# First block of a two-block model: retention heads and neighbourhood-attention heads in pairs, decay blocks made once, weight rounding in two halves

## The reference, cut to what matters

```
proj = hn @ w_in                      # rq rk rv rg nq nk nv, 512 columns each
rq, rk = rotary(rq), rotary(rk) / 8
y   = retention(rq, rk, rv)           # 8 heads of 64: (q k^T) * gamma^|i-j|, one gamma
                                      # forwards, one backwards, times v
y   = group_norm(y) * g * silu(rg)
na  = neighbourhood_attention(nq, nk, nv, bias)   # 8 heads of 64, softmax over 256 keys
out = concat(y, na) @ w_out
```

## Time and profile before

| | |
|---|---|
| median of 3 runs | 1109.04 us (1108.8 to 1109.66) |
| the profiled execution: time, span | 1107.25 us, 1105.5 us |
| TensorE busy, weight loads | 1022.7 us (93%), 897.2 us |
| VectorE, ScalarE, GpSimd busy | 519.2, 607.8, 688.2 us |
| mean granted TensorE clock | 0.960 of 2.4 GHz |
| DMA | 178.68 MB, 162 GB/s in the mean |

### The profile page before, as it was taken

One profiled execution on the slowest core, in us unless ns is written; L12 is line 12 of the kernel. 1 busy time (PEld: TensorE's weight loads), 2 busy tenths in 40 slices (PEclk: granted clock), 3 DMA queues, 4 the chain that ended last, 5 costly groups with the idle time before them and its releaser, 6 DMA issues. The chain is left out here.

```text
span 1105.5 us, 16084 instructions
## 1 busy us (share of the span) xinstructions
PE 1022.7 (93%) x6261; PEld 897.2 (81%) x6261; DVE 519.2 (47%) x988; ACT 607.8 (55%) x969; POOL 688.2 (62%) x546
## 2 busy tenths in 40 slices
PE   5999797999999899899988689999997999999988
PEld 4897576999999688788867579999996887787877
DVE  3934614545444546386752545545444225114443
ACT  6443535655555566586845455555556467755531
POOL 3976324665757477676746655665675963866464
PEclk9999688999999899899988789999998999999999
DMA  9773212666454465554523345555455654743320
GB/s 320 242 211 131 98 39 86 225 231 230 163 191 150 130 191 158 188 168 155 192 95 118 130 134 191 174 189 200 162 189 160 155 189 150 231 132 135 116 76 38
DMA packets 131945, 178.68 MB, mean 162 GB/s; under 512 B 21457, under 2 KB 94045, under 8 KB 131677
## 3 DMA queue, kind: packets, MB, share of 16 engines
q1 hardware_dynamic: 127693, 169.95, 47.2%
q10 hardware_dynamic: 4176, 7.71, 2.2%
HBM read 176.51 MB, written 5.24 MB: 164 GB/s over the span
## 5 line engine op out<-in xcount | busy, mean ns | idle before, releaser
L496 POOL TENSOR_TENSOR wlo<-raw,whi 128x512 fp32r<-128x512 f32 x510 | 668.5, 1346 | 399.6 <-ACT whi L1123 399.6
L1123 ACT ACTIVATE whi<-raw 128x2048 fp32r<-128x2048 f32 (+1 forms) x150 | 283.5, 1893 | 191.1 <-PE PS L513 134.2
L511 PE MATMUL PS<-Th,whi 128*128 128x256 f32 (+1 forms) x1008 | 289.9, 288 | 2.8 <-POOL wlo L496 1.4
L512 PE MATMUL PS<-Tl,whi 128*128 128x256 f32 (+1 forms) x1008 | 287.3, 285 | 0.0
L513 PE MATMUL PS<-Th,wlo 128*128 128x256 f32 (+1 forms) x1008 | 287.1, 285 | 0.0
L508 PE MATMUL PS<-whi,Th 128*128 128x512 f32 (+1 forms) x512 | 208.7, 408 | 13.1 <-DVE Tl L1615 6.2
L510 PE MATMUL PS<-whi,Tl 128*128 128x512 f32 (+1 forms) x512 | 201.7, 394 | 0.0
L509 PE MATMUL PS<-wlo,Th 128*128 128x512 f32 (+1 forms) x512 | 201.6, 394 | 0.0
L511 PEld LDWEIGHTS PS<-Th,whi 128*128 128x128 f32 (+1 forms) x1008 | 194.1, 193 | 8.8 <-issue 4.1
L1670 DVE SCALAR_TENSOR_TENSOR arena<-PS,cols,arena 128x255 f32<-128x255 f32 (+1 forms) x272 | 118.6, 478 | 168.0 <-ACT arena L1222 155.2
L512 PEld LDWEIGHTS PS<-Tl,whi 128*128 128x128 f32 (+1 forms) x1008 | 194.3, 193 | 1.3 <-issue 0.5
(11 more groups left out here) (216 smaller groups left out, 1117.1 us busy)
## 6 DMA issues: line engine op xcount, KB each, us to landing
raw<-in_ffn_w_up_dram SPq DMA_DIRECT2D x44, 1024.0 KB, 5.1
raw<-in_ffn_w_down_dram SPq DMA_DIRECT2D x22, 1024.0 KB, 4.9
raw<-in_w_in_dram SPq DMA_DIRECT2D x22, 1024.0 KB, 5.0
raw<-in_c_w_in_dram SPq DMA_DIRECT2D x16, 1024.0 KB, 5.3
raw<-in_ab_w_in_dram SPq DMA_DIRECT2D x14, 1024.0 KB, 7.3
raw<-in_c_w_out_dram SPq DMA_DIRECT2D x8, 1024.0 KB, 4.9
raw<-in_ab_w_out_dram SPq DMA_DIRECT2D x4, 1024.0 KB, 4.9
raw<-in_c_w_in_dram SPq DMA_DIRECT2D x8, 512.0 KB, 5.3
```

What stands on the lines that cost most here:

```text
L496: i = nc.gpsimd.tensor_tensor(wlo[n % NLO][:, c:e], raw[n % NRAW][:, c:e], whi[n % NHI][:, c:e].bitcast(F32), ALU.subtract)
L511: mm(o, wh, ah, start=first, stop=False)
L512: mm(o, wh, al, start=False, stop=False)
L1123: act.activation(whi[n % NHI][:, 0:width], raw[n % NRAW][:, 0:width], ACT.Copy)\
```

## The change

1. Slots: `rg` comes before `nv`; the NA bias loads go ahead of slot `nv 0`, which is one place later in SyncE's queue. `rg` is made in banks 2 and 3, `nv` in 0 and 1.
2. `high(n)` rounds in two instructions of half a slot each; the first signals `w_hi_half`, on which GpSimd starts the first half of its subtractions.
3. Retention in pairs: the scores of two heads are sent alternately, half a `fm` slot follows (`halves`), then both outputs. VectorE multiplies each head in two operations of 256 columns.
4. The decay blocks of all heads are made once: the 128x128 blocks off the diagonal by 16 exponentials on ScalarE with a scale from a column, the diagonal ones by three wide VectorE operations and three exponentials. They lie in free room of the arena, in `sqj` and in `gpost`, so the load of `gpost` moves behind the retention.
5. NA with the function `pairs` of the second block, made general: scores of two heads alternately, then hooks with half or whole slots (`nv`, `mo0`), then transposes and values. The gate of the retention output is worked out before NA as far as it does not need `rg`. The NA output is turned in two parts (`turn_na`), the second inside `out_last`.

```diff
-        tm("nv", win, 3072)
         tm("rg", win, 1536)
+        tm("nv", win, 3072)
...
-                if n == slot_no[("nv", 1)]:
+                if n == slot_no[("nv", 0)]:
...
-                pool.wait_ge(*at("w_hi", n))
+                pool.wait_ge(*at("w_hi_half", n))
...
+                step = min(512, width // 2)
+                for c in range(0, width, step):
+                    e = c + step
+                    if c == width // 2:
+                        pool.wait_ge(*at("w_hi", n))
...
-            for h in range(NH + 1):
-                if h < NH:
-                    ret_scores(h)
-                if h >= 1:
-                    ret_out(h - 1)
-                if h == 1:
-                    slot_fm(("nq", 1), 3)
-                elif h in (2, 3):
-                    slot_fm(("nk", h - 2), h - 2)
-                elif h in (4, 5):
...
+            for p in range(NH // 2):
+                ret_scores(p)
+                if p < 2:
+                    slot_fm(("nq", 1), 3, halves=(p,))
+                else:
+                    if p == 2:
+                        pe.wait_ge(*read(("rv", 1)))
+                    slot_fm(("nk", 0), 0, halves=(p - 2,))
+                ret_out(2 * p)
+                ret_out(2 * p + 1)
+            slot_fm(("nk", 1), 1)
+            pe.wait_ge(*read(("nq", 1)))
+            block_tm("rg", 2)
...
+                for p in range(n + 1):                       # pairs, TensorE
+                    if p < n:
+                        if p:
+                            pe.wait_ge(*at("a_sc", (tag, 2 * p - 1)))
+                        for t in range(NT):
+                            for i in (2 * p, 2 * p + 1):
+                                o = mm(PS[:, 4 + i % 2, ...], q(t), k(nk), start=True, stop=True)
+                        hook(p, "a")
+                        turn(2 * p)
+                    if p:
+                        values(2 * p - 2)
+                        values(2 * p - 1)
+                    if p < n:
+                        hook(p, "m")
+                        turn(2 * p + 1)
+                    hook(p, "b")
...
+                  keyed({(0, "a"): (lambda: na_value(0),), (0, "b"): (lambda: na_value(1), turn_ret), (1, "a"): (mo_first,),
+                         (2, "a"): (lambda: out_slot("mo0", 1, 10, ("y0a", 3), halves=(0,)),),
+                         (3, "a"): (lambda: out_slot("mo0", 1, 10, ("y0a", 3), halves=(1,)),),
+                         (3, "b"): (lambda: turn_na(0),)}))
+            out_last("mo0", 4, (12, 14), [("y0b", 1), ("y0b", 3)], mid=lambda: turn_na(2))
...
-                    act.activation(whi[n % NHI][:, 0:width], raw[n % NRAW][:, 0:width], ACT.Copy)\
-                        .then_inc(*done("w_hi", n))
+                    hf = width // 2
+                    act.activation(whi[n % NHI][:, 0:hf], raw[n % NRAW][:, 0:hf], ACT.Copy).then_inc(*done("w_hi_half", n))
+                    act.activation(whi[n % NHI][:, hf:width], raw[n % NRAW][:, hf:width], ACT.Copy).then_inc(*done("w_hi", n))
...
+            for h, (a, b) in enumerate(dcy_at):              # ScalarE, behind set_up
+                act.activation(dcy3[a][:, b, 0:P], pfb[:, 1, S:S + P], ACT.Exp, scale=lg[:, 8 + h:9 + h])
+                i = act.activation(dcy3[a][:, b, S:S + P], pfb[:, 0, P:S], ACT.Exp, scale=lg[:, h:h + 1])
...
+            for a, h, n in ((0, 0, 5), (1, 5, 1), (2, 6, 2)):
+                act.activation(dcy3[a][:, :, P:S], darg[0][:, h:h + n, :], ACT.Exp).then_inc(*done("r_d", a))
...
+            pairs("na", 4, False, keyed({                    # ScalarE; U(x) rounds up to three slots behind x
+                (0, "m"): (U(("nv", 0)),), (0, "b"): (value_copy, U(("nv", 1)), lambda: T_hi("y0a", 4, 8, 2, lambda k: col("gn", k))),
+                (1, "m"): (U(("mo0", 0)),), (3, "m"): (U(("mo0", 1)),), (3, "b"): (lambda: T_hi("y0b", 2, 12, 4, lambda k: None),)}))
...
-                lk(ts(dcy[h % 2], pfb[:, 1, :], lg[:, 8 + h:9 + h], None, ALU.mult))
-                stt3(out=dcy[h % 2], in0=pfb[:, 0, :], scalar=lg[:, h:h + 1], in1=dcy[h % 2], op0=ALU.mult, op1=ALU.add)\
-                    .then_inc(*done("r_arg", h))
...
+            for k in range(2):
+                i = tt(darg[k], bc(pfb[:, 1 - k, 0:P], 1, NH), bc(lg[:, 8 - 8 * k:16 - 8 * k], 2, P), ALU.mult)
+            lk(i)
+            tt(darg[0], darg[0], darg[1], ALU.add).then_inc(*done("r_arg"))
...
+            ret_var()
+            ret_scale()
+            pairs("na", 4, False, lambda i, t: nabias[:, i, 128 - 128 * t:384 - 128 * t], na_write,
+                  keyed({(0, "a"): (ret_gate,), (1, "x"): (lambda: T_lo("y0a", 4, 8, 2, lambda k: col("gn", k)),),
+                         (3, "b"): (lambda: T_lo("y0b", 2, 12, 4, lambda k: None),)}))
```

More of the change, by code:

```diff
@@ L547, in slot_fm, with slot_dn @@
                                   k == 0, k == KD - 1, False)
-                i.then_inc(*done("w_used", n))
-            def slot_dn(name, ah, al, first, b0=4, mid=None):
+                if 1 in halves:
+                    i.then_inc(*done("w_used", n))
+            def slot_dn(name, ah, al, first, b0=4, mid=None, halves=(0, 1)):
                 n = slot_no[name]
-                pe.wait_ge(*low(n))
+                if 0 in halves:
+                    pe.wait_ge(*low(n))
                 h, l = whi[n % NHI], wlo[n % NLO]
-                order = [(k, t, hf) for k in range(2) for t in range(NT) for hf in range(2)]
+                order = [(k, t, hf) for k in halves for t in range(NT) for hf in range(2)]
                 for j, (k, t, hf) in enumerate(order):
@@ L561, in slot_dn, with last_two @@
                               first and k == 0, False, True)
[L562 to L564 removed]
+                if 1 in halves:
+                    i.then_inc(*done("w_used", n))
+            def last_two(names, acts, ready, b0=4, mid=None):
                 ns = [slot_no[name] for name in names]
@@ L731, in values @@
-                    n.then_inc(*done("a_v", (tag, i)))
-                n = len(heads)
-                for i in range(n + 2):
-                    if i < n:
-                        scores(i)
-                    if 1 <= i <= n:
-                        turn(i - 1)
-                    if i >= 2:
-                        values(i - 2)
-                    after(i)
-            def operands(h, qT, kT, kk, v, causal):
-                b = (h % 2) * DH
-                return (lambda t: qT[b:b + DH, h // 2, t * P:(t + 1) * P], lambda nk: kT[b:b + DH, kk, 0:nk], v, causal)
@@ L747, in _ @@
-            pe.wait_ge(*read(("nv", 1)))
-            pe.wait_ge(*at("gn_c", 1))
-            def also(table):
-                def f(i):
-                    for g in table.get(i, ()):
-                        g()
-                return f
+                        for c in range(t + 1 if causal else NT):
+                            a = (i // 2 % 2) * 256 + t * P + (i % 2) * DH
+                            o = mm(PS[:, 7, a:a + DH], pt[i % 2][:, 2 * t + c, :], heads[i][2](c), start=c == 0, stop=c == (t if causal else NT - 1))
@@ new lines, in keyed, with f, operands, na_value @@
+            def keyed(table):
+                def f(p, place):
+                    for g in table.get((p, place), ()):
+                        g()
+                return f
+            def operands(h, qT, kT, kk, v):
+                b = (h % 2) * DH
+                return (lambda t: qT[b:b + DH, h // 2, t * P:(t + 1) * P], lambda nk: kT[b:b + DH, kk, 0:nk], v)
+            def na_value(hf):
+                if hf == 0:
+                    pe.wait_ge(*read(("nk", 1)))
+                slot_tm(("nv", hf), 0, 4 * hf, hf == 0, hf == 1)
@@ L1327, in also @@
-            def also(table):
-                def f(i):
-                    for g in table.get(i, ()):
-                        g()
-                return f
-            def later(name):
-                return lambda: high(slot_no[name] + 3)
-            high(slot_no[("rg", 1)] + 3)
-            attention("na", NH, False, also({0: (ret_gate,), 3: (lambda: T_hi("y0a", 4, 8, 0, lambda k: col("gn", k)),), 5: (later(("mo0", 0)),),
-                                             8: (later(("mo0", 1)),)}))
@@ L1821, in ret_var, with keyed, f, na_write @@
+            def keyed(table):
+                def f(p, place):
+                    for g in table.get((p, place), ()):
+                        g()
+                return f
+            def na_write(p, rc, o):
+                return tt(hn[:, :, 512 + P * p:512 + P * (p + 1)].rearrange("p t (h d) -> p t h d", h=2), o, bc(rc, 3, DH), ALU.mult)
             def ret_var():
```

444 lines of the change are left out of this document (173 added, 271 removed).

## The result

The changed kernel takes 1083.97 us (median of 4 runs, 1082.29 to 1086.53); beside it the kernel before took 1109.35 us (1108.8 to 1109.76). The ratio is 0.9767, 95% interval 0.9739 to 0.9794: 25.4 us less. I use these two where sizes matter: 25.2 us. By this median the time lies just inside the range, so that the miss of its end is small; the 19.8 us of gain were short by 5.4 all the same.

What follows compares the result with a forecast made beforehand. TensorE was taken to set the time, waiting in the first block's NA. 0.4 + 2.8 + 18.2 - 2.5 + 0.9 = 19.8 us off the median of 1109.04 gave 1089.3 us, range 1084.5 to 1097.0.

Steps and rivals of the forecast that it cites:

- Net elsewhere: gain 0.9: Rounding in halves, beyond the start: 2.4 us less waiting for GpSimd against 1.5 us of later roundings; bounds -2 and +2.4.
- 0.4 us at the start: Rounding in halves: TensorE's 0.48 us wait for GpSimd at 22.58 us goes, minus 0.1 us for VectorE's first slot.
- retention: Retention in pairs: 3.15 us fewer scores and a 0.77 us wait gone, less a 1.1 us stall: gain 2.8 us.
- NA and its clock (18.2 - 2.5): NA in pairs: 11.6 us idle, 4.2 scores and 7.5 low clock removed, 5.1 new idle added; 2.5 lost to the clock.
- the new gap: NA, near 118 us: TensorE stands 3.5 us for ScalarE and VectorE; the clock falls to 1.2 GHz, 2.5 us lost.
- The mask stall: Retention, third pair: VectorE's two masks while GpSimd works make TensorE wait 1.1 us; bounds 0 and 2.2.
- (1): NA: the clock does not fall in the 3.5 us gap, 2.5 us more gain: 1086.8 us, chance 0.15.
- (2): Retention: ScalarE is late, with decay exponentials of 0.5 us and masks under GpSimd's work: 1094.3 us, chance 0.16.
- (3): NA: the clock stays low through the pairs until 140 us, costing 8.5 instead of 2.5 us: 1095.3 us, chance 0.06.
- (4): Retention and NA scores: interleaved pairs don't run side by side, price 7.4 us: 1096.7 us, chance 0.04.
- (5): Slots after the first block: halves make ScalarE the bound, 0.2 us on each, and the kernel slower: 1115.1 us, chance 0.03.
- (6): Slots behind the change: the gain is given back as they wait for rounding or loads: 1109 us, chance 0.02.

Runs made afterwards that it cites:

- whole roundings: The changed kernel with each slot rounded in one ScalarE instruction again, run in two groups: 1087.99 us by median.
- gate ahead: The changed kernel with NA heads singly in the old order, the retention output's gate still worked out before NA: 1096.75 us.
- gate inside: The changed kernel with single NA heads and the retention output's root, tanh copies and gating products put back inside NA: 1104.1 us.
- doubled exponentials: The changed kernel with the sixteen 128x128 exponentials of the decay blocks issued twice, with the same values: 1085.46 us.
- Halves only up to layer 1: The changed kernel with slots rounded in halves only before the first slot of the state-space layer, whole from there on: 1086.94 us.
- high parts first: The changed kernel with ScalarE's four high parts of the retention output moved ahead of the next slot's rounding: 1081.14 us.

## Why the forecast was off, step by step

**What failed: "Net elsewhere: gain 0.9" of the rounding in halves,** and with it the assumption that beyond NA nothing moves but idle time. With the 0.4 us at the start the forecast gave the halves 1.3 us; they are worth 3.3 us on the changed kernel and 3.6 on the one before. I had counted both sides as idle time: waits for GpSimd (up to 2.4) against roundings ahead of a wait (1.5). Both sides were too small. The runs show 5.0 us for the second operation alone and 5.6 to 8.3 us for the earlier start, with TensorE's idle time the same within 1.1 us. What moves beside it is the time at 1.2 GHz. The rest of the change was short as well: the kernel before against whole roundings makes 21.9 us (interval 19.7 to 23.6), and the forecast's terms without the halves 18.5. The bounds -2 and +2.4 stood on idle time as well, so the range was too narrow at this point.

**The ladder.** By medians: before 1109.9; halves 1106.3 (-3.6); retention in pairs, decay blocks once and the order of slots 1104.1 (-2.2); gate ahead of NA 1096.75 (-7.35); NA in pairs 1084.7 (-12.1).

| step | forecast | by medians | by the two timelines |
|---|---|---|---|
| halves (0.4 + 0.9) | 1.3 | 3.6 | 1.2 at the start |
| retention | 2.8 | 2.2 | 4.4 |
| NA and its clock (18.2 - 2.5) | 15.7 | 19.4 (12.8 to 21.0) | 15.9 |
| behind 157 us | (in the 0.9) | | -0.8 |

The last column compares the profiled executions of before and after: the retention's first scores start at 59.38 and 58.18 us; from there to NA's first scores it is 55.91 and 40.56 us, and from these to the end of the projection 63.28 and 58.31 us. The two value slots, 10.9 us (48 products in steps of 0.2275), lie in the first part before and in the second after, and are moved. It adds up to 20.7 us.

*The NA term* was right in size by the timelines (15.9) and named one thing too few. The forecast credits the 11.6 us of idle time and 7.5 us of clock to pairs. 7.35 us of it by medians is the move of the gate: the 3.85 us gap of the earlier trace rows was ScalarE's root and tanh with their two table loads, and behind it the clock stayed low. Pairs alone, without the move, are not tried. By medians the size is 3.7 us over the forecast, inside its interval. The clock behind the new gap fell for 3.4 us, so that the 5.7 us slot took 7.35 us, 1.6 lost where I took 2.5; the rest over 15.9 is low clock elsewhere, as below.

*The reading of the clock* was wrong in one point. The forecast has the clock halve behind the 3.85 us gap, and takes the fall in its own gap from the gap's length (2.28 us left it alone, 4.14 didn't). In the kernel before the clock falls at 120.3 us, 0.2 us after that gap began, as in the experiments above; and the runs show falls right behind gaps of 1.68, 1.88 and 2.27 us and none behind one of 3.60. A fall did come where it was forecast, in two of three profiles of the changed kernel: that it was the profiled one is in part luck.

*Retention.* The scores are 1.13 us per pair as forecast, and the 0.77 us wait is gone. The mask stall is 0.19 us at 75.13, where I took 1.1: the two masks took 2.67 us, and the product ended earlier. The 2.2 us by medians has an interval of -0.3 to 8.6, and the kernel behind it (gate inside) has a wait of 1.17 us for the copy of the values ahead of NA's first scores, which neither the one before nor the changed one has; the timelines say 4.4 us, 1.6 over the forecast, 0.9 of it the mask. The start gained 0.92 us against whole roundings (1.85 to 0.92), where I read 0.48 from the earlier trace rows: in that execution the first slot ran slowly and had hidden part of the wait.

*The place and the whole.* Up to 157.05 us the profiled execution has gained 21.5 us, forecast 18.9; the 2.6 between are 1.6 in the retention, 0.8 at the start and 0.2 in NA, where 0.9 less lost to the clock stands against 0.7 in other terms. Behind it nothing is gained in that execution (last product 1101.68 and 1080.94, 20.7). The other 4.5 us up to the 25.2 are between executions: from the 54 and 16 executions, (1-c) times the time fell by 45.7 - 31.8 = 13.9 us, while the profiled NA stretch accounts for (23.9 - 3.4)/2 = 10.3 of it. The 3.6 us left lie in low clock outside NA, which no term of the sum had; the runs don't show how much of them is the halves. I had anchored the clock on one execution of before that was itself below the median of its kind by 2.7 us (1107.25 to 1109.91).

**The rivals.** (1) The clock does fall in the profiled execution, 1.3 us behind the gap of 3.60 us, but not in every one: the next profiled execution of the same kernel has a gap of 3.60 us there too and 1.00 behind it. Of the rivals it comes nearest in time (1086.8). (2) ScalarE late in the retention: no wait at all; the doubled exponentials show about 4 us of room. (3) The clock low through the pairs: 3.4 us, not 19. The Trainium skill ("TensorE: Matmul & The Clock Gate", Part 4) says that transposes do not count as work for the clock as matmuls do. Behind the gap of 3.79 us the attention work with its transposes did not lift the clock in 13.5 us (120.85 to 134.31), which agrees with that rule; but in the version with the gate ahead the same work left a clock of 1.00 where it was, so that the transposes alone did not make it fall. (4) Side by side: eight records in 1.13 us. (5) Not slower: the second operation costs 5.0 us without the early start, with it the halves gain. (6) Nothing was given back.

**Open.** Why a second rounding operation, or GpSimd's 0.86 us earlier start, changes the time at 1.2 GHz outside the start. Between 566 and 584 us whole roundings had 10.2 us at the low clock in both profiles and halves 3.4 us in all three, with gaps of the same sum to 0.1 us (2.79 + 2.06 and 1.95 + 2.84), so the place of the gaps may decide. Halves only up to layer 1, where the roundings are whole at this place, have 10.2 us and the gaps of whole ones. At 392 us it is the other way round: with halves one gap of 2.27 us and then 3.4 or 6.8 us at 1.2 GHz, with whole roundings two gaps of some 1.35 us, 19 us apart, and no fall. No edit here moved one such gap by itself.

## What to carry to other kernels

Before an idle stretch is credited to the loop that it lies in, look at what the releasing engine did in it: here a root and a tanh with two table loads of 1.28 us between two heads made the gap behind which the clock stayed low, and moving them was worth 7.4 of 19.4 us by medians. Look at the clock in fine steps too: it had fallen before or as this gap began, so that the gap prolonged the low stretch and didn't start it. A single gap of TensorE costs its length and what the clock does around it; of the two versions that shortened one gap of 3.6 us, the one that only reordered three operations on ScalarE gave 3.5 us. Where several per cent of the time are spent at 1.2 GHz, an edit that leaves the idle time alone can still move the time by 3 to 5 us, so an estimate from idle time needs a range of that width, and its base is several executions, not the profiled one.

## What the runs showed of the hardware

- Executions of one kernel differ in how often TensorE is at 1.2 GHz: the kernel before had mean clocks of 0.954 to 0.963 and 1105.9 to 1118.6 us, its longest at 0.954 and its shortest at 0.963.
- The length of a gap of TensorE doesn't tell by itself whether the clock falls. It fell right behind gaps of 1.68 us (decay exponentials twice, at 61 us), 1.88 us (whole roundings, at 22 us) and 2.27 us (changed kernel, at 392 us); it stayed at 1.00 behind gaps of 1.70 us (high parts first, at 118 us) and 2.38 us (changed kernel, at 1045 us), and behind the gap of 3.60 us of the changed kernel in one profile of three.
- The first matrix products can run slowly with the granted clock read as 1.00. The changed kernel in its second profile (0.63 us each up to 18.93) and in its first (0.39 to 0.40 us):

```profile
15.52 0.63 PE L515 MATMUL PS<-wlo,Th 128*128 128x512 f32 x1
...
18.93 0.43 PE L514 MATMUL PS<-whi,Th 128*128 128x512 f32 x1
```

```profile
15.11 0.40 PE L515 MATMUL PS<-wlo,Th 128*128 128x512 f32 x1
```

  The slow start costs 9 x 0.2 = 1.8 us, of which about 0.9 is hidden, since it takes the place of the wait for GpSimd at 21 us (0.92 us).
- Cutting a ScalarE operation of 1.90 us in two of 1.04 and 1.05 us, used for nothing, cost 5.0 us over 150 slots, though its extra time (0.08 to 0.1 us per slot) hardly shows in TensorE's gaps (71.5 us in all, against 72.2 with whole roundings).
